# Three seven-product steps instead of two in the first seven column pairs, with the banks joined through transfers

## The chip, the cores and the metric

The kernel runs on one core of one Trainium2 chip. The metric is the device time of one execution in microseconds (us). Three executions of the kernel before took 2105.9 to 2107.35 us, with a median of 2106.39 us.

## The reference

The program is two transformer-like layers on 256 tokens of width 2048, in float32. The change touches only the first large projection, `proj = einsum('bsd,dn->bsn', rms_norm(x, norm_g), w_in)`: of its columns, the second half of `v_a`, then `o_a` and `z_a` (which gate the mLSTM output as `sigmoid(o_a) * h_a * silu(z_a)`), and `z_b` (used as `silu(z_b)`). Everything else (the remaining columns, the mLSTM, the attention, the Fourier mix, the MLP) is the same before and after.

## The kernel before

**Stream and pieces.** All weights arrive as a stream of units, each 128 partitions by 2048 columns (1 MB), through a ring of four buffers `raw` (SyncE, L477 to L479: unit u is asked for when the first two pieces of unit u-4 are split). A unit is cut into pieces of 1024 columns. ScalarE rounds a piece to the format that TensorE reads (`w_hi`, `split`, L1203), VectorE subtracts (`w_lo`, `split`, L1747), and TensorE multiplies activations with both: three matmuls of 128x512 for each product (`hi*hi`, `hi*lo`, `lo*hi`; `product`, L732 to L734). `w_hi` and `w_lo` have four places. Piece n may be rounded only when TensorE is done with piece n-4 (`act.wait_ge(w_used, ...)`, L1201). So ScalarE and VectorE are at most four pieces ahead of TensorE.

**Column pairs.** Seven pairs of 1024 columns each (`pair_in`, PAIRS_IN = 7) are computed in eight steps. One step is one unit, that is two k-tiles by two column halves, for two token tiles: eight block products. A plain step (`plain_step`, L742) has two pieces of 12 matmuls, 24 in all. A special step (`sum_step`, L754) is a Winograd step: seven products, 21 matmuls, in four pieces of 6, 3, 6 and 6 matmuls. The last step (`end_step`, L775) is plain, but ordered by bank. The results of a pair lie in four banks called whole and four called mixed; the roles swap from pair to pair (`parts_in`, L337). `SUM_AT_IN` says where the special steps are: steps 3 and 5 in pairs 1 to 4, steps 2 and 5 in pairs 0, 5 and 6.

**What a special step costs beside TensorE.** VectorE adds weights before it: `sum_weights` (L1753) makes one add of 1024 columns (L1761) and two of 512 (L1764, L1765), into one of two buffers `w_sum`. It is called inside `split`, directly after the first piece of the unit before. The special unit then has four pieces (1024, 512, 1024, 1024 columns) to round and to subtract, where a plain one has two of 1024. The sums of the activations (`xs_hi`, `xs_lo`) are made once, in the stage before (`sum_x`, `round_x_sums`, `rest_of_x_sums`).

**Joins.** In the step after the last special one, ScalarE copies the first mixed bank into `joined` (L1359) and VectorE makes four adds there (`join_mixed`, L2006 to L2011, two in each slot). At the end of the pair VectorE adds the four whole banks as they come (`join_whole`, L2023). In step 0 of the next pair ScalarE and VectorE turn `joined` into results (`take`): for pair 0 four scaled copies (`take_v`), for pairs 1 to 4 four sigmoids (L1326, L1328) and two pairs of VectorE products (`take_o`, L1977, L1978), for pairs 5 and 6 four sigmoids (L1337) and four products (`take_z`, L1989), where the sigmoids of the second half wait for the products of the first.

**Order.** Each engine works through its queue in program order. A `slot(j)` is run behind piece j's turn in the loop, and because the split is four pieces ahead, the slot of (step s, piece j) stands behind the split of the piece four further on. In this text piece s.j is piece j of step s of a pair. In pair 0 there are two extra slots: a table load and two sines on ScalarE at step 0 (L1351, L1352), and `rope_k` on VectorE at step 3 (L1844 to L1855). GpSimd (the POOL queue) has nothing to do during the pairs; behind them it stores `z1` (L509).

## Time and profile before

| | |
|---|---|
| median of three executions | 2106.39 us (2105.9 to 2107.35) |
| the profiled execution | 2106.43 us |
| its span, first to last instruction | 2104.2 us |
| granted TensorE clock | 0.999 of full |
| TensorE matmuls, busy | 2085.2 us, x10059 |
| VectorE busy | 1442.1 us |
| ScalarE busy | 1084.4 us |
| GpSimd busy | 39.6 us |

The span leaves 2.2 us of the profiled execution's time outside it. Matmuls overlap: one lasts 0.39 us from start to end while the next starts 0.23 us behind it, so the starts and not the busy time tell the pace. A column "[idle before <-releaser]" gives the time that the engine waited before an instruction and the work that ended the wait. In the timeline, "x3" is a run of three instructions shown as one, with the time from the first's start to the last's end.

### The profile page before, as it was taken

To read this page: it belongs to the slowest core of one execution; us is meant where nothing else is said; L and a number is where in the kernel's file an instruction comes from. 1 tells how busy PE (TensorE), PEld (TensorE's weight loads), DVE (VectorE), ACT (ScalarE), POOL (GpSimd) and SP (SyncE) were. 2 spreads that over 40 slices of the span, in tenths; PEclk is the share of its full clock that TensorE was granted. 3 is DMA by queue.
4 is the path that set the end of the run, shared out by engine and by line. 5 is a ranking of instruction groups with operands and counts; after the bars stand their busy time and mean duration, and the time that the engine had idled before them with its cause. 6 is when DMAs were issued, how large, how long until landed. Compare 5 with 4: busy or idle time off the path is not lost.

```text
span 2104.2 us, 24976 instructions
## 1 busy us (share of the span) xinstructions
PE 2085.2 (99%) x10059; PEld 1751.8 (83%) x10059; DVE 1442.1 (69%) x1872; ACT 1084.4 (52%) x1412; POOL 39.6 (2%) x49
## 2 busy tenths in 40 slices
PE   8999999999999999999999999999999999999998
PEld 6888888888888888888888888888888888888886
DVE  5977788875555786556554455466896796796684
ACT  5455555555444675554454454354544554454453
POOL 0000000000000020000000000000000000000000
PEclk9999999999999999999999999999999999999999
DMA  7555555564565544365755542455555465456562
GB/s 273 180 196 188 196 200 202 188 244 185 180 224 197 182 158 160 140 221 199 296 184 187 188 160 101 162 198 190 195 207 189 169 232 183 178 199 220 183 220 98
DMA packets 56803, 402.60 MB, mean 191 GB/s; under 512 B 6256, under 2 KB 6640, under 8 KB 9584
## 3 DMA queue, kind: packets, MB, share of 16 engines
q1 hardware_dynamic: 53648, 380.61, 50.3%
q0 software_dynamic: 2608, 19.66, 2.4%
q8 instruction: 80, 1.31, 0.3%
q10 hardware_dynamic: 432, 0.73, 0.1%
q14 instruction: 35, 0.29, 0.0%
HBM read 392.59 MB, written 8.39 MB: 191 GB/s over the span
## 4 chain that ended last, share of the span: by engine, by line
PE 96%; DVE 1%; ACT 1%; issue 1%; DMA 0%; SPq 0%; POOLq 0%; POOL 0%; DVEq 0%; ACTq 0%
PE proj L619 15%; PE proj L621 15%; PE proj L620 15%; PE proj L1092 11%; PE proj L1096 6%; PE proj L732 4%; PE proj L734 4%; PE proj L733 4%; PE tbank L732 2%; PE tbank L733 2%; PE tbank L734 2%; PE tbank L578 2%; PE bank_a L732 1%; PE bank_a L734 1%; PE bank_a L733 1%; PE bank_b L732 1%
## 5 line engine op out<-in xcount | busy, mean ns | idle before, releaser
L1747 DVE TENSOR_TENSOR w_lo<-raw,w_hi 128x1024 fp32r<-128x1024 f32 x630 | 747.1, 1200 | 517.0 <-ACT w_hi L1203 509.5
L1203 ACT ACTIVATE w_hi<-raw 128x1024 fp32r<-128x1024 f32 x630 | 647.9, 1040 | 745.7 <-PE proj L621 466.2
L619 PE MATMUL proj<-w_hi,a_both 128*128 128x512 f32 x1280 | 512.6, 401 | 0.0
L621 PE MATMUL proj<-w_hi,a_both 128*128 128x512 f32 x1280 | 500.3, 391 | 0.0
L620 PE MATMUL proj<-w_lo,a_both 128*128 128x512 f32 x1280 | 499.0, 390 | 0.0
L621 PEld LDWEIGHTS proj<-w_hi,a_both 128*128 128x128 f32 x1280 | 240.5, 188 | 51.8
L620 PEld LDWEIGHTS proj<-w_lo,a_both 128*128 128x128 f32 x1280 | 241.0, 188 | 47.5
L619 PEld LDWEIGHTS proj<-w_hi,a_both 128*128 128x128 f32 x1280 | 241.0, 188 | 47.0
L1092 PE MATMUL proj<-a_both,w_hi 128*128 128x512 f32 x672 | 160.6, 391 | 0.3 <-DVE a_both L1793 0.3
L1092 PEld LDWEIGHTS proj<-a_both,w_hi 128*128 128x128 f32 x672 | 123.5, 188 | 24.5 <-DVE a_both L1793 0.5
L1203 ACT ACTIVATE w_hi_deep<-raw 128x1024 fp32r<-128x1024 f32 x84 | 83.6, 1021 | 95.1 <-PE proj L1096 59.5
L1747 DVE TENSOR_TENSOR w_lo_deep<-raw,w_hi_deep 128x1024 fp32r<-128x1024 f32 x84 | 97.1, 1177 | 44.4 <-ACT w_hi_deep L1203 44.1
L1096 PEld LDWEIGHTS proj<-a_both,w_lo 128*128 128x128 f32 x672 | 86.3, 191 | 3.4
L1096 PE MATMUL proj<-a_both,w_lo 128*128 128x256 f32 x672 | 87.3, 283 | 0.0
L1092 PE MATMUL proj<-a_both,w_hi_deep 128*128 128x512 f32 x352 | 84.1, 391 | 0.0
L1092 PEld LDWEIGHTS proj<-a_both,w_hi_deep 128*128 128x128 f32 x352 | 64.7, 188 | 12.6
L732 PE MATMUL proj<-w_hi,a_both 128*128 128x512 f32 x164 | 64.0, 391 | 0.1
L733 PE MATMUL proj<-w_lo,a_both 128*128 128x512 f32 x164 | 63.8, 389 | 0.0
L734 PE MATMUL proj<-w_hi,a_both 128*128 128x512 f32 x164 | 63.8, 389 | 0.0
L1096 PEld LDWEIGHTS proj<-a_both,w_lo_deep 128*128 128x128 f32 x352 | 45.3, 191 | 1.8
L619 PE MATMUL proj<-w_hi,lat_hi 128*128 128x512 f32 x112 | 45.7, 408 | 0.3 <-DVE v_b L2251 0.3
L1096 PE MATMUL proj<-a_both,w_lo_deep 128*128 128x256 f32 x352 | 45.8, 283 | 0.0
(524 smaller groups left out, 2999.3 us busy)
## 6 DMA issues: line engine op xcount, KB each, us to landing
raw<-stream SPq DMA_DIRECT2D x358, 1024.0 KB, 4.8
nat<-x SPq DMA_DIRECT2D x4, 512.0 KB, 9.6
z_store<-z POOLq DMA_DIRECT2D x1, 2048.0 KB, 8.4
ga_store<-z POOLq DMA_DIRECT2D x1, 2048.0 KB, 12.1
gb_store<-z POOLq DMA_DIRECT2D x4, 512.0 KB, 7.2
yb<-z_store POOLq DMA_DIRECT2D x4, 512.0 KB, 9.6
ga<-ga_store POOLq DMA_DIRECT2D x1, 2048.0 KB, 8.1
gb<-gb_store POOLq DMA_DIRECT2D x1, 2048.0 KB, 14.3
```

Of the source, the lines that this page charges most:

```text
L578: last = nc.tensor.transpose(tbank[(tr.n - aside.n) % 2][:, b * P:(b + 1) * P], src(b), ident)
L619: nc.tensor.matmul(banks[t][:, :], ah, wh, start=first, stop=False)
L620: nc.tensor.matmul(banks[t][:, :], ah, wl, start=False, stop=False)
L621: last = nc.tensor.matmul(banks[t][:, :], al, wh, start=False, stop=end)
L732: nc.tensor.matmul(bank[:, :], hi, wh, start=first, stop=False)
L733: nc.tensor.matmul(bank[:, :], hi, wl, start=False, stop=False)
L734: return nc.tensor.matmul(bank[:, :], lo, wh, start=False, stop=end)
L1092: nc.tensor.matmul(banks[f], hi_places[place_of(piece.n + i)][:, cols], a_both[:, kt, :, :].rearrange("p s t -> p (s t)"), start=(kt == 0) ...
L1096: last = nc.tensor.matmul(banks[f][:, 0:TOK], lo_places[place_of(piece.n)][:, cols], a_hi[:, kt, :], start=False, stop=(kt == KT - 1))
L1203: A(hi_places[s][:, 0:width], src, ACT.Copy).then_inc(w_rounded, 1)
L1747: V.tensor_tensor(lo_places[s][:, 0:width], src, hi_places[s][:, 0:width].bitcast(f32), SUB).then_inc(w_rest, 1)
```

## The change

There are three special steps in each of the seven pairs, at steps 1, 3 and 5, and a third set of activation sums, made in the second `v` projection before the pairs. `w_sum` has one buffer instead of two during the pairs. The mixed banks are joined in one go in step 5 (the slot of its third piece): ScalarE waits for all four pieces of the step, copies one bank, and VectorE makes the four additions, now with signs such that the whole banks need only be added. `join_whole` is gone from VectorE. In its place ScalarE copies the four whole banks into `stg` and `stg2` (`drain_pair`), and GpSimd issues four transfers that add these to `joined` in memory (`accum_op=ADD`), 28 in all. The `take` of the pair before moves from step 0 to step 2 on ScalarE, where it waits for the four transfers, and on VectorE to step 2 (second slot, first half) and step 4 (first slot, second half). Behind the last pair it moves from pieces 0 and 1 of the next projection to pieces 3 and 4. The diff, with repeated hunks (the removed waits on `whole_added` in `take_o` and `take_z`, the indexing of `xs_hi` and `xs_lo`) left out:

```diff
...
 PAIRS_IN = 7
-GROUPS_IN = (1, 4)
-SUM_AT_IN = [(2, 5)] + [(3, 5)] * 4 + [(2, 5)] * 2
-ORDER_IN = [(0, 2, 1, 3, 5, 4, 6, 7) if at[0] == 2 else (0, 2, 3, 1, 5, 4, 6, 7) for at in SUM_AT_IN]
+GROUPS_IN = (1, 4, 5)
+SUM_AT_IN = [(1, 3, 5)] * PAIRS_IN
+ORDER_IN = [(0, 1, 2, 4, 3, 5, 6, 7)] * PAIRS_IN
 def _sum_units():
...
 SUM_UNITS = _sum_units()
-SUMS_IN = 2 * PAIRS_IN
+SUMS_IN = len(GROUPS_IN) * PAIRS_IN
 def _pieces():
...
         joined = place("joined", [P, 4, CW], f32, 152.25)
-        w_sum_vo = place("w_sum_vo", [P, 2, 2 * PIECE], f32, 160.25)
-        w_sum_z = place("w_sum_z", [P, 2, 2 * PIECE], f32, 176.25)
+        xs_hi_2 = place("xs_hi_2", [P, 4, P], f32r, 176.25)
+        xs_lo_2 = place("xs_lo_2", [P, 4, P], f32r, 178.25)
+        xs_hi = [xs_hi[:, 0], xs_hi[:, 1], xs_hi_2[:, :, :]]
+        xs_lo = [xs_lo[:, 0], xs_lo[:, 1], xs_lo_2[:, :, :]]
+        w_sum_vo = place("w_sum_vo", [P, 2 * PIECE], f32, 160.25)
+        w_sum_z = place("w_sum_z", [P, 2 * PIECE], f32, 184.25)
...
         at += 8
+        drain_in = {2: stg[:, 0, :], 3: stg[:, 1, :], 0: stg2[:, 0, :], 1: stg2[:, 1, :]}
...
         def w_sums(i):
-            if i < 2 * 5:
-                return w_sum_vo[:, i % 2, :]
-            return (w_sum_z if i < SUMS_IN else w_sum)[:, i % 2, :]
+            if i < SUMS_IN:
+                return (w_sum_vo if i < len(GROUPS_IN) * 5 else w_sum_z)[:, :]
+            return w_sum[:, i % 2, :]
         def par_c(name, i=0):
...
         m_copied = sem("m_copied")
-        whole_added = sem("whole_added")
+        joined_in = [sem(f"joined_in{o}") for o in range(4)]
...
+            for p in range(PAIRS_IN):
+                for i, o in enumerate(END_ORDER):
+                    pool.wait_ge(part_read, 5 * p + 2 + i)
+                    pool.dma_start(joined[:, o, :], drain_in[o], accum_op=ADD).then_inc(joined_in[o], 16)
...
             def take_v(p, n):
-                act.wait_ge(whole_added, 4 * (p + 1))
                 for t in range(TT):
...
             def take(p, n):
                 if p >= 0:
+                    if n == 0:
+                        for o in END_ORDER:
+                            act.wait_ge(joined_in[o], 16 * (p + 1))
                     (take_v if p < 1 else take_o if p < 5 else take_z)(p, n)
...
+            def drain_pair(p):
...
+                act.wait_ge(part_read, 5 * p + 1)
+                if p == 0:
+                    act.wait_ge(qk_ready, 8)
+                act.wait_ge(gated, tiles.at(2))
+                for i, o in enumerate(END_ORDER):
+                    if i < 3:
+                        act.wait_ge(part_done, 3 * p + i + 1)
+                    else:
+                        act.wait_ge(w_used, done.at(RING + 2))
+                    A(drain_in[o], parts_in[p % 2][o][:, :], ACT.Copy).then_inc(part_read, 1)
             def pair_in(p):
...
                             A(cos[:, :, :], cos[:, :, :], ACT.Sin).then_inc(trig, 1)
-                        if step == 0:
+                        if step == 2:
                             take(p - 1, j)
-                        if step == SUM_AT_IN[p][-1] + 1 and j == 0:
-                            act.wait_ge(w_used, done.at(RING))
+                        if step == SUM_AT_IN[p][-1] and j == 2:
+                            act.wait_ge(w_used, done.at(RING + 4))
...
                             A(joined[:, 0, :], parts_in[1 - p % 2][0][:, :], ACT.Copy).then_inc(m_copied, 1)
+                    if step == STEPS - 1:
+                        drain_pair(p)
...
                 chunk.add(2)
...
+            def last_x_sums(j):
+                if j == 6:
+                    act.wait_ge(qk_ready, 8)
+                    round_x_sums(2)
...
             for i in range(2):
-                pieces(slot=(lambda j: (conv_slot(j), exp_slot(j))) if i == 0 else lambda j: exp_slot(8 + j))
+                pieces(slot=(lambda j: (conv_slot(j), exp_slot(j))) if i == 0 else lambda j: (exp_slot(8 + j), last_x_sums(j)))
                 for t, b in enumerate(banks()):
...
             for i in range(2):
                 def lat_slot(j, i=i):
-                    if i == 0 and j < 2:
-                        take(PAIRS_IN - 1, j)
-                    if i == 0 and j == 4:
+                    if i == 0 and 3 <= j < 5:
+                        take(PAIRS_IN - 1, j - 3)
+                    if i == 0 and j == 7:
                         act.wait_ge(gated, tiles.at(2))
+                        act.wait_ge(proj_read, chunk.at() * 2)
...
                 s = w_sums(i).rearrange("p (b c) -> p b c", b=4)
-                if i > 1:
-                    dve.wait_ge(w_rest, FIRST_PIECE[SUM_UNITS[i - 2]] + 4)
+                reader = i - (1 if i < SUMS_IN else 2)
+                if reader >= 0 and (i < SUMS_IN) == (reader < SUMS_IN):
+                    dve.wait_ge(w_rest, FIRST_PIECE[SUM_UNITS[reader]] + 4)
...
-            def take_o(n):
...
-                if n == 0:
-                    return
+            def take_o(t):
...
                 i = tiles.n // 2
-                for t in range(TT):
-                    tiles.add()
-                    dve.wait_ge(sig, tiles.at())
-                    chain(V.tensor_tensor(stg2[:, t, :], stg2[:, t, :], stg[:, t, :], MUL))
-                    V.scalar_tensor_tensor(nat[:, t, i * CW:(i + 1) * CW], joined[:, 2 * t + 1, :], inv1[:, t:t + 1],
-                                           stg2[:, t, :], MUL, MUL).then_inc(gated, 1)
-                    dve.wait_ge(gated, tiles.at(2))
-                    dve.sem_inc(proj_read, 1)
+                tiles.add()
+                dve.wait_ge(sig, tiles.at())
+                chain(V.tensor_tensor(stg2[:, t, :], stg2[:, t, :], stg[:, t, :], MUL))
+                V.scalar_tensor_tensor(nat[:, t, i * CW:(i + 1) * CW], joined[:, 2 * t + 1, :], inv1[:, t:t + 1],
+                                       stg2[:, t, :], MUL, MUL).then_inc(gated, 1)
+                dve.wait_ge(gated, tiles.at(2))
+                dve.sem_inc(proj_read, 1)
             def take_z(n):
...
-            def take(p, n):
+            def take(p, half):
                 if p >= 1:
-                    (take_o if p < 5 else take_z)(n)
+                    (take_o if p < 5 else take_z)(half)
             def join_mixed(p, part):
...
                     chain(V.tensor_tensor(m[:, 2, :], mixed[2][:, :], m[:, 0, :], ADD))
-                    V.tensor_tensor(m[:, 1, :], mixed[1][:, :], m[:, 2, :], ADD).then_inc(dve_seq, 1)
+                    V.scalar_tensor_tensor(m[:, 1, :], mixed[1][:, :], -1.0, m[:, 2, :], MUL, SUB).then_inc(dve_seq, 1)
...
                 else:
-                    chain(V.tensor_tensor(m[:, 2, :], mixed[3][:, :], m[:, 2, :], ADD))
-                    V.tensor_tensor(m[:, 3, :], mixed[1][:, :], m[:, 2, :], ADD).then_inc(part_read, 1)
...
-            def join_whole(p):
...
-                whole = parts_in[p % 2]
-                dve.wait_ge(dve_seq, seq.at())
-                dve.wait_ge(part_read, 5 * p + 1)
-                for i, o in enumerate(END_ORDER):
-                    if i < 3:
-                        dve.wait_ge(part_done, 3 * p + i + 1)
-                    else:
-                        dve.wait_ge(w_used, done.at(RING + 2))
-                    V.tensor_tensor(joined[:, o, :], whole[o][:, :], joined[:, o, :],
-                                    SUB if o in (1, 2) else ADD).then_inc(part_read, 1)
-                dve.wait_ge(part_read, 5 * p + 5)
-                dve.sem_inc(whole_added, 4)
+                    dve.wait_ge(dve_seq, seq.at())
+                    chain(V.scalar_tensor_tensor(m[:, 2, :], mixed[3][:, :], -1.0, m[:, 2, :], MUL, SUB))
+                    V.tensor_tensor(m[:, 3, :], mixed[1][:, :], m[:, 2, :], SUB).then_inc(part_read, 1)
             def pair_in(p):
...
                     def slot(j):
...
                             rope_k()
-                        if step == 0:
-                            take(p - 1, j)
-                        if step == at[-1] + 1:
-                            join_mixed(p, j)
-                    if step == STEPS - 1:
-                        join_whole(p)
+                        if step == 2 and j == 1:
+                            take(p - 1, 0)
+                        if step == 4 and j == 0:
+                            take(p - 1, 1)
+                        if step == at[-1] and j == 2:
+                            join_mixed(p, 0)
+                            join_mixed(p, 1)
...
                 gates_slot(8 * i + j)
+                if i == 1 and j == 5:
+                    sum_x(2)
+                if i == 1 and j == 7:
+                    rest_of_x_sums(2)
...
             for i in range(2):
                 def lat_slot(j, i=i):
-                    if i == 0 and j < 2:
-                        take(PAIRS_IN - 1, j)
-                        if j:
+                    if i == 0 and 3 <= j < 5:
+                        take(PAIRS_IN - 1, j - 3)
+                        if j == 4:
...
```

## Rows read from the trace of the kernel before

**Rows 1.** The page: engines, and the chain that ended last

```profile
PE 2085.2 (99%) x10059; PEld 1751.8 (83%) x10059; DVE 1442.1 (69%) x1872; ACT 1084.4 (52%) x1412; POOL 39.6 (2%) x49
...
PE 96%; DVE 1%; ACT 1%; issue 1%; DMA 0%; SPq 0%; POOLq 0%; POOL 0%; DVEq 0%; ACTq 0%
```

**Rows 2.** Busy time by stretch, each about one pair (columns in the first line)

```profile
core 0: us, PE busy (x) PEld busy (x) DVE busy (x) ACT busy (x) POOL busy (x), PEclk, DMA share, GB/s
...
284.00:326.00 42.00, 41.93 (x185) 34.41 (x184) 34.91 (x38) 22.98 (x25) 0.00 (x0) 1.00 0.52 195
326.00:369.00 43.00, 42.93 (x189) 35.21 (x188) 35.92 (x40) 22.97 (x25) 0.00 (x0) 1.00 0.53 200
```

**Rows 3.** Waits from 200 to 455 us: total us, times, longest

```profile
DVE w_lo L1747 <- ACT w_hi L1203: 38.9, 34, 2.5
ACT w_hi L1203 <- PE bank_b L734: 17.8, 4, 4.4
ACT stg L1337 <- DVE z L1989: 2.8, 1, 2.8
```

**Rows 4.** TensorE's timeline: first of 49 matmuls without gap, then a gap

```profile
297.09 0.39 PE L734 MATMUL proj<-w_hi,a_both 128*128 128x512 f32 x1
...
307.97 0.39 PE L734 MATMUL proj<-w_hi,a_both 128*128 128x512 f32 x1
308.43 0.50 PE L732 MATMUL proj<-w_hi,a_both 128*128 128x512 f32 x1
308.77 0.39 PE L733 MATMUL proj<-w_lo,a_both 128*128 128x512 f32 x1
309.00 0.39 PE L734 MATMUL proj<-w_hi,a_both 128*128 128x512 f32 x1
```

**Rows 5.** Idle time in front of TensorE's L732, 200 to 700 us

```profile
  DVE w_lo L1747: 2.3, 5
```

**Rows 6.** VectorE's timeline in pair 2, with the take of pair 1

```profile
292.20 1.22 DVE L1747 TENSOR_TENSOR w_lo<-raw,w_hi 128x1024 fp32r<-128x1024 f32 x1
293.33 0.69 DVE L1977 TENSOR_TENSOR stg<-stg,stg 128x512 f32<-128x512 f32 x1
294.06 0.75 DVE L1978 SCALAR_TENSOR_TENSOR nat<-joined,inv,stg 128x512 f32<-128x512 f32 x1
294.95 0.69 DVE L1977 TENSOR_TENSOR stg<-stg,stg 128x512 f32<-128x512 f32 x1
...
304.57 1.22 DVE L1761 TENSOR_TENSOR w_sum_vo<-raw 128x1024 f32<-128x1024 f32 x1
...
307.16 2.96 DVE L1747 TENSOR_TENSOR w_lo<-raw,w_hi 128x1024 fp32r<-128x1024 f32 x3
...
314.00 4.63 DVE L1747 TENSOR_TENSOR w_lo<-raw,w_hi 128x1024 fp32r<-128x1024 f32 x4
320.12 1.23 DVE L1747 TENSOR_TENSOR w_lo<-raw,w_hi 128x1024 fp32r<-128x1024 f32 x1 [1.49 <-ACT w_hi L1203]
321.26 0.69 DVE L2006 TENSOR_TENSOR joined<-tbank,joined 128x512 f32<-128x512 f32 x1
321.98 0.69 DVE L2007 TENSOR_TENSOR joined<-bank_b,joined 128x512 f32<-128x512 f32 x1
...
325.43 2.48 DVE L2023 TENSOR_TENSOR joined<-proj,joined 128x512 f32<-128x512 f32 x4
```

**Rows 7.** ScalarE's timeline in the same pair

```profile
288.34 1.32 ACT L1326 ACTIVATE stg<-joined,inv 128x512 f32<-128x512 f32 x2
...
302.33 3.10 ACT L1203 ACTIVATE w_hi<-raw 128x1024 fp32r<-128x1024 f32 x3 [0.30 <-PE proj L734]
...
308.45 1.06 ACT L1203 ACTIVATE w_hi<-w_sum_vo 128x1024 fp32r<-128x1024 f32 x1 [2.14 <-PE proj L734]
...
319.99 0.58 ACT L1359 ACTIVATE joined<-bank_a 128x512 f32<-128x512 f32 x1
```

**Rows 8.** The extra slots of pair 0: ScalarE's table load, VectorE's rope

```profile
163.47 1.28 ACT L1351 ACT_TABLE_LOAD   x1
164.76 0.26 ACT L1351 ACTIVATE sin<-sin 128x64 f32<-128x64 f32 x1
164.92 0.24 ACT L1352 ACTIVATE cos<-cos 128x64 f32<-128x64 f32 x1
...
179.04 0.29 DVE L1844 TENSOR_TENSOR kr<-sm 128x128 f32<-128x128 f32 x1
...
181.32 0.69 DVE L1747 TENSOR_TENSOR w_lo<-raw,w_hi 128x512 fp32r<-128x512 f32 x1
```

**Rows 9.** VectorE's timeline, 459 to 465 us: take behind the last pair

```profile
459.19 1.64 DVE L1989 SCALAR_TENSOR_TENSOR z<-joined,inv,stg 128x512 f32<-128x512 f32 x2
460.98 1.22 DVE L1747 TENSOR_TENSOR w_lo<-raw,w_hi 128x1024 fp32r<-128x1024 f32 x1
...
464.00 1.23 DVE L1747 TENSOR_TENSOR w_lo<-raw,w_hi 128x1024 fp32r<-128x1024 f32 x1 [0.24 <-DVE z L1989]
```

**Rows 10.** A GpSimd issue; transfers by line (KB each, us to landing)

```profile
464.22 0.58 POOL L509 DMA_DIRECT2D z_store<-z  x1 [431.74 <-DVEq L2065]
...
raw<-stream SPq DMA_DIRECT2D x358, 1024.0 KB, 4.8
...
gb_store<-z POOLq DMA_DIRECT2D x4, 512.0 KB, 7.2
yb<-z_store POOLq DMA_DIRECT2D x4, 512.0 KB, 9.6
...
out<-nat SPq DMA_DIRECT2D x2, 256.0 KB, 2.9
```

More of the change, by code:

```diff
@@ L804, in pair_in @@
                         i = at.index(step)
-                        sum_step(kt, whole, mixed, a_hi, a_lo, xs_hi[:, i], xs_lo[:, i], i + 1, i == 0, i == len(at) - 1)
+                        sum_step(kt, whole, mixed, a_hi, a_lo, xs_hi[i], xs_lo[i], i + 1, i == 0, i == len(at) - 1)
                     elif step == STEPS - 1:
@@ L1291, in round_x_sums @@
                 act.wait_ge(ms_summed, i + 1)
-                A(xs_hi[:, i, :, :], xs[:, :, :], ACT.Copy).then_inc(ms_rounded, 1)
+                A(xs_hi[i], xs[:, :, :], ACT.Copy).then_inc(ms_rounded, 1)
             def k_slot(j, i):
@@ L1320, in take_o @@
             def take_o(p, n):
-                act.wait_ge(whole_added, 4 * (p + 1))
                 for t in range(TT):
@@ L1332, in take_z @@
             def take_z(p, n):
-                act.wait_ge(whole_added, 4 * (p + 1))
                 for t in range(TT):
@@ L1953, in rest_of_x_sums @@
                 dve.wait_ge(ms_rounded, i + 1)
-                V.tensor_tensor(xs_lo[:, i, :, :], xs[:, :, :], xs_hi[:, i, :, :].bitcast(f32), SUB).then_inc(ms_rest, 1)
+                V.tensor_tensor(xs_lo[i], xs[:, :, :], xs_hi[i].bitcast(f32), SUB).then_inc(ms_rest, 1)
             def k_slot(j, i):
```

## The prediction

> **What bounds the kernel now.** I read the page first. TensorE is busy for 99% of the span and is 96% of the chain that ended last [rows 1]. That does not yet say that it never waits, since matmuls overlap, so the second view is the busy time by stretch: in a stretch of one pair VectorE is busy 35 to 36 of 42 to 43 us, ScalarE 23, and the transfers 53% [rows 2]. The third is the table of waits: almost all waits of ScalarE are on TensorE and those of VectorE on ScalarE, and both are harmless, since they only mean that the ring of four pieces is full [rows 3]. The last are the timelines. TensorE starts a matmul every 10.88 / 48 = 0.2267 us [rows 4]. A plain step is then 24 x 0.2267 = 5.44 us, a piece of it 2.72, a special step 21 x 0.2267 = 4.76 (pieces of 1.36, 0.68, 1.36, 1.36).
>
> TensorE does wait in a few places: five times, 2.3 us with the 0.2267 us of pace that each gap between starts contains [rows 5], so 2.3 - 5 x 0.2267 = 1.2 us, and 0.11 more each for the restart (0.34 where the pace is 0.23) [rows 4]. One such gap is from 307.97 to 308.43, behind w_lo of the second piece of plain step 4, which stands between special steps 3 and 5. VectorE could not start that piece before 307.16, since the weight sums of step 5 (from 304.57, 2.59 us) stand in front of it [rows 6]. So **a plain step between two special ones already costs TensorE 0.23 + 0.11 = 0.34 us**. The change makes two such places in each pair and puts further work in them.
>
> **What is removed.** One plain step in seven pairs becomes special: 7 x 3 matmuls x 0.2267 = 4.76 us. The four gaps of pairs 1 to 4 and a small one in pair 6 go too, as pieces of the old order: 4 x 0.34 + 0.15 = 1.5 us. Both together, 6.3 us, are what can be gained. VectorE loses four adds at the pair's end (2.48 us) [rows 6]. They hold up nothing: VectorE waits for ScalarE right behind them [rows 3], so their end gains nothing by itself.
>
> **What is added, piece by piece.** Lengths: ScalarE starts a rounding 0.25 us behind TensorE's end of the piece it waits for (308.45 against 307.97 + 0.2267) and takes 1.06, or about 1.01 with another behind it [rows 7]. VectorE takes 1.23 behind a wait, 1.14 in a row (4.63 = 3 x 1.14 + 1.22), 2.59 for the three sums [rows 6]. From its end to TensorE's next matmul I take 0.09; the gap at 308.43 against 307.16 + 1.23 shows 0.04 [rows 4, 6], and I add as much for the hops between the queues.
>
> (a) *Step 2, behind special step 1, pairs 1 to 6.* From TensorE's end of piece 1.0: 0.25 + 1.06 (ScalarE, 2.0) + 1.14 (VectorE, 2.0) + 2.59 (sums for step 3) + 1.23 (VectorE, 2.1) + 0.09 = 6.36. TensorE has 0.68 + 1.36 + 1.36 + 2.72 = 6.12 us of work. Missing: 0.24, with the restart 0.35, which is the gap seen before. Six times: 2.1 us.
>
> (b) *Step 4, behind special step 3, pairs 2 to 5.* Piece 3.3 may be rounded when TensorE ends 2.1. VectorE's queue then holds 3.3, the first tile of the moved take (0.73 + 0.89 = 1.62, from 293.33 to 294.95 [rows 6]), 4.0, the sums for step 5, and 4.1. Piece 4.0: 0.25 + 1.06 + 1.14 + 1.62 + 1.23 + 0.09 = 5.39 against 4.76 of step 3: 0.63 + 0.11. Then 4.1 needs 2.59 + 1.14 = 3.73 behind 4.0, while TensorE works on 4.0 for 2.72: another 1.01. Together 1.75, four times: 7.0 us. In pair 1 the take is ScalarE's alone (1.32 [rows 7] between 3.3 and 4.0): 0.25 + 1.01 + 1.32 + 1.06 + 1.23 + 0.09 = 4.96, so 0.31 + 1.01 = 1.3 us.
>
> (c) *Pair 0.* The table load and the sines (163.47 to 165.16, 1.7 us [rows 8]) stand behind the split of 1.3, in front of 2.0. From TensorE's end of 0.1: 0.25 + 1.01 + 1.7 + 1.06 + 1.23 + 0.09 = 5.34 against 4.76, so 0.69, and 1.01 for 2.1: 1.7 us. rope_k (179.04 to 181.32, 2.28 us) stands behind the sums for step 5, in front of 4.1: 0.24 + 2.28 + 0.11 = 2.6 us.
>
> (d) *Pair 6.* Here ScalarE's second pair of sigmoids waits for VectorE's first two products, as it already did once for 2.8 us with plain pieces as cover [rows 3]. From the end of 2.1: 0.25 + 1.06 + 1.14, two products (1.79, from 459.19 to 460.98 [rows 9]), two sigmoids 1.34, then 4.0 on ScalarE 1.06 and VectorE 1.23, 0.09: 8.0 against 4.76, so 3.3 us with the restart, and again 1.01 for 4.1: 4.3 us.
>
> (e) *The join.* ScalarE's wait for the whole of step 5 costs nothing, since its next piece needs the same. The copy (0.58) and four VectorE operations (0.72 each, 321.26 to 321.98 [rows 6, 7]) stand in front of the second piece of step 7, with 5.44 us of step 6 as cover. With VectorE some 0.5 us behind at that point I get 5.6: about 0.13 a pair, 0.9 us in all, and nothing if VectorE has caught up.
>
> (f) *The drain.* Four ScalarE copies lie where ScalarE idled 4.4 us [rows 3]. The last delays piece 1.0 of the next pair: 0.25 + 0.64 + 1.06 + 1.23 + 0.09 = 3.3 us against the 5.44 of step 0: covered. So are the third activation sums, in plain pieces with 1.5 us of idle VectorE each [rows 6]. The single sum buffer adds no wait, its readers stand earlier in VectorE's own queue. If that cover went, each would cost its excess only.
>
> (g) *The transfers.* No row shows one that adds. ScalarE needs them behind its rounding of 3.2, which waits for TensorE's end of 2.0: 5.44 + 4.76 + 2.72 + 0.25 + 1.01 = 14.2 us behind the pair's end; and the last is issued by 1.6 us (0.9 for the drained bank, 0.6 to 0.7 for the issue), so it has 12.6 us. The nearest plain ones take 2.9 us (256 KB) and 7.2 to 9.6 (512 KB, from GpSimd) [rows 10]. I take something between, 5 us, which costs nothing, with the ends zero and what rival B gives. Weight transfers land in 4.8 us and have some 13 us, so contention must nearly treble that to matter. One row speaks on whether VectorE keeps GpSimd from issuing: its issue at 464.22 took 0.58 us while VectorE ran a w_lo from 464.00 to 465.23, and neither is longer than usual [rows 9, 10].
> The Trainium skill, page "SBUF — State Buffer", section "SBUF: two separate sides", states that GpSimd writes the descriptors of its transfers and can be shut out while VectorE runs a two-port operation; with the page's 3.1 us instead of 0.62 for an issue, four would end near 13 us and the joins would come at the limit, which would add rival B's time. That trace row does not agree, though it is one issue.
>
> **Sum.** 2.1 + 7.0 + 1.3 + 1.7 + 2.6 + 4.3 + 0.9 = 19.9 us added, 6.3 removed: 13.6 us slower. The profiled execution took 2106.43 us (span 2104.2, 2.2 outside), the median is 2106.39, so the same base: **2120 us**. The terms' own uncertainty, 0.1 us for each of 28 stops, the 0.9 of (e), and a third of (c) and (d), gives 2115 to 2125.
>
> **Rivals.** A, *not slower: the takes are hidden.* Everything hangs on whether VectorE's work between TensorE's end of 2.1 and the end of w_lo of 4.1 (9.1 us in pairs 2 to 5) fits in 7.5 us. If it did, because the queue is further ahead than my count of four pieces says, only the bare gap would stay: 14 x 0.35 - 1.5 - 4.76 = -1.4, 2105.0 us. For it: VectorE's work in a pair, 3 x 4.0 + 5 x 2.28 (splits) + 3 x 2.59 (sums) + 2.9 (join) + 3.2 (take) = 37.3 us, is less than the pair's 5 x 5.44 + 3 x 4.76 = 41.5; and the takes cost nothing before. Against it: the ring of four is a wait in the code, and the bare gap is in the trace. If the bare gap were hidden as well, -4.8 - 1.5 gives 2100.1 us, *faster*. B, *joins arrive late.* If the last transfer takes 16 us instead of under 12.6, ScalarE stands 3.4 us in each of six pairs in front of the stall that is already there: +20 us, 2140. For it: four transfers at once among 200 GB/s of weights, a second read for the sum. Against: every GpSimd row of 512 KB lands under 10 us. C, *the gain is smaller than 21 matmuls*, because a special step issues some other way: the same code runs in 14 steps of the trace, so under 1 in 100.
>
> **How the numbers follow.** Forecast 0.74; A with only the takes hidden 0.09; all hidden 0.05; B 0.12. Two tenths of a per cent (4.2 us) is about what a measurement of this kernel tells from no change. The forecast and B are slower by more, A is within it, all hidden is faster: 0.05, 0.09, 0.86. The range takes in the forecast's own 2115 to 2125, on the low side a case in which three fifths of what (b) to (d) add beyond seven bare gaps (16.9 - 2.4 = 14.5 us) is hidden (2111), on the high side the half of B that is late by under 2 us (2130). Left out are A's two cases and the later half of B, 0.2.
>
> **What would show it.** 21 fewer TensorE matmuls than 10059. A pair's length from its last drained bank to the next's: about 45.9 (pair 0), 43.3, 43.7 four times, 46.4 (pair 6) instead of 42.5 or 42.1. VectorE's w_lo as the releaser of TensorE's L732 in some 28 places instead of 5, the longest (3 us) in pair 6 and (2.5 us) at rope_k. ScalarE's idle time in front of the takes released by TensorE, not by a DMA; if a DMA stands there, B holds. Pairs of 41.5 us and no more than 5 gaps would make the prediction wrong.

## The result, and the profile after

The changed kernel took 2122.18 us (median of 4 runs, 2121.81 to 2122.63) beside 2106.8 us for the kernel before on the same chip (4 runs, 2105.9 to 2107.35): a ratio of 1.0074, with a 95% interval from 1.0062 to 1.0086. That is 15.4 us slower; 13.6 were forecast, and 2122.18 lies in the range. The profiled execution took 2122.63 us, of which the span is 2120.7. Of the executions of the last batch below, two of the kernel before and two of e11 were slow ones, at 2555 to 9618 us, and its medians are those of the others.

The page of the changed kernel: the engines' busy time, the chain that ended last, and two of its DMA issues (KB each, median us to landing).

```profile
PE 2089.1 (99%) x10038; PEld 1748.5 (82%) x10038; DVE 1455.6 (69%) x1885; ACT 1110.3 (52%) x1455; POOL 63.4 (3%) x77
...
PE 93%; DVE 3%; ACT 2%; issue 2%; DMA 0%; SPq 0%; POOLq 0%; DVEq 0%; POOL 0%; ACTq 0%
...
raw<-stream SPq DMA_DIRECT2D x358, 1024.0 KB, 4.8
joined<-stg POOLq DMA_DIRECT2D x28, 256.0 KB, 7.4
```

TensorE issues 21 matmuls fewer than in [rows 1], as the change says, and still its busy time has grown by 3.9 us. Part of the chain has moved from TensorE to VectorE and ScalarE: from 1% each to 3% and 2%. Transfers have 0% of it.

Where TensorE stops is told by the idle time in front of L741, the first matmul of each triple. For the same stretch as [rows 5] (200 to 700 us) the row is the first below; the second fence has the waits from 160 to 470 us, all seven pairs (us in total, times, longest).

```profile
  DVE w_lo L1777: 26.9, 34
```

```profile
ACT w_hi L1212 <- PE tbank L743: 58.7, 35, 5.9
DVE w_lo L1777 <- ACT w_hi L1212: 50.9, 35, 3.0
...
PEld bank_a L741 <- DVE w_lo L1777: 14.0, 11, 3.3
PE bank_a L741 <- DVE w_lo L1777: 9.1, 8, 2.9
...
PEld proj L741 <- DVE w_lo L1777: 8.0, 12, 1.1
...
PE proj L741 <- DVE w_lo L1777: 3.2, 6, 0.7
...
ACT stg L1343 <- DVE z L2017: 2.9, 1, 2.9
...
PEld tbank L741 <- DVE w_lo L1777: 0.9, 4, 0.2
```

The first two rows only say that the ring is full, as in [rows 3]. A longer stop is listed twice, once in front of the weight load (PEld) and once in front of the matmul (PE). The weight loads alone are 11 + 12 + 4 = 27 stops, against 5 before. They sum to 22.9 us, less 27 x 0.2267 us of pace, 16.8 us. No row names a DMA.

The stops themselves, as the distance between starts less 0.2267 us, come from TensorE's timeline. Behind each stop the next start is 0.11 us late as well (the restart), so a stop is written as 0.63 + 0.11. Around pair 3, whose like before had no stop but the one in [rows 4]:

```profile
305.28 0.39 PE L743 MATMUL proj<-w_hi,a_both 128*128 128x512 f32 x1
305.74 0.50 PE L741 MATMUL proj<-w_hi,a_both 128*128 128x512 f32 x1
...
314.00 0.50 PE L741 MATMUL proj<-w_hi,a_both 128*128 128x512 f32 x1 [0.47 <-DVE w_lo L1777]
...
317.72 0.50 PE L741 MATMUL proj<-w_hi,a_both 128*128 128x512 f32 x1 [0.70 <-DVE w_lo L1777]
```

The first is at piece 2.1 (0.23 us, and 0.11 more behind the next matmul for the restart), the second at 4.0 (0.63 + 0.11, with the matmul before it at 313.14), the third at 4.1 (0.86 + 0.11, matmul before at 316.63). VectorE's timeline shows what stood in front of the two later ones:

```profile
309.95 1.23 DVE L1777 TENSOR_TENSOR w_lo<-w_sum_vo,w_hi 128x1024 fp32r<-128x1024 f32 x1 [1.39 <-ACT w_hi L1212]
311.10 0.68 DVE L2005 TENSOR_TENSOR stg<-stg,stg 128x512 f32<-128x512 f32 x1
311.82 0.75 DVE L2006 SCALAR_TENSOR_TENSOR nat<-joined,inv,stg 128x512 f32<-128x512 f32 x1
312.72 1.23 DVE L1777 TENSOR_TENSOR w_lo<-raw,w_hi 128x1024 fp32r<-128x1024 f32 x1
313.86 1.22 DVE L1792 TENSOR_TENSOR w_sum_vo<-raw 128x1024 f32<-128x1024 f32 x1
315.11 0.69 DVE L1795 TENSOR_TENSOR w_sum_vo<-w_sum_vo,raw 128x512 f32<-128x512 f32 x1
315.84 0.69 DVE L1796 TENSOR_TENSOR w_sum_vo<-w_sum_vo,raw 128x512 f32<-128x512 f32 x1
```

The split of 3.3, the moved take (two operations), the split of 4.0, the sums for step 5, and only then the split of 4.1, from 316.44: the queue that step (b) of the prediction wrote down.

Two stops are longer, at rope_k in pair 0 and at the sigmoids of pair 6. Busy time by stretch around them (columns in the first line). The first row is the stop at rope_k, the second the 4.3 us behind it, the third the time after that, the fourth the 4.3 us behind the stop of pair 6; the last is pair 3 as a whole, which answers to [rows 2]:

```profile
core 0: us, PE busy (x) PEld busy (x) DVE busy (x) ACT busy (x) POOL busy (x), PEclk, DMA share, GB/s
181.00:184.60 3.60, 1.28 (x6) 0.74 (x4) 3.36 (x12) 1.06 (x1) 0.00 (x0) 1.00 0.00 0
184.70:189.00 4.30, 4.30 (x12) 3.40 (x13) 2.75 (x3) 0.00 (x0) 0.00 (x0) 0.61 0.77 272
189.10:193.00 3.90, 3.90 (x19) 3.19 (x18) 2.39 (x3) 3.27 (x4) 0.00 (x0) 1.00 0.58 231
447.60:451.90 4.30, 4.30 (x12) 3.39 (x13) 4.23 (x5) 1.08 (x2) 0.00 (x0) 0.60 0.00 0
283.40:327.10 43.70, 42.45 (x184) 34.02 (x183) 36.98 (x40) 26.50 (x31) 3.40 (x4) 1.00 0.66 216
```

In pair 3 TensorE now idles for 1.25 of 43.70 us, where [rows 2] have 0.07. The column PEclk is what the prediction did not have: over the 4.3 us behind each stop the granted clock is 0.6 in the mean (it is 0.50 from 185.7 to 189.0 us, while the slow matmuls run), and 12 matmuls fit in 4.3 us where 19 fit in 3.9 us a moment later. The timeline has it matmul by matmul:

```profile
181.89 0.39 PE L743 MATMUL tbank<-w_hi,a_both 128*128 128x512 f32 x1
184.63 0.50 PE L741 MATMUL bank_a<-w_hi,a_both 128*128 128x512 f32 x1 [2.36 <-DVE w_lo L1777]
184.98 0.40 PE L742 MATMUL bank_a<-w_lo,a_both 128*128 128x512 f32 x1
...
185.70 0.63 PE L742 MATMUL bank_b<-w_lo,a_both 128*128 128x512 f32 x1
186.13 0.63 PE L743 MATMUL bank_b<-w_hi,a_both 128*128 128x512 f32 x1
186.56 0.63 PE L741 MATMUL tbank<-w_hi,a_both 128*128 128x512 f32 x1
```

A stop of 2.51 us, four matmuls at the old pace, and then eight with 0.43 us between starts instead of 0.2267: 8 x 0.2 = 1.6 us more. The slow spacing is that of the lower of the two levels, 1.2 GHz instead of 2.4 (512 / 1.2 GHz = 0.427 us). This is one reason why PE's busy time grew; the longer first matmul behind each stop (0.50 us instead of 0.39) is another.

**The account.** What all distances between starts in the seven pairs have over 0.2267 us, slow matmuls included, sums to 22.8 us in the changed kernel and to 1.6 in the kernel before. With 4.76 us for the removed matmuls the pairs are 16.4 us longer. The two profiled spans differ by 16.5 us (2120.7 and 2104.2), so outside the pairs the time is the same within 0.2 us; the medians differ by 15.4. Of the 22.8 us the rows below hold 22.0; the other 0.8 is in distances that are less than 0.05 us too long each.

| step of the prediction | forecast, us | found, us |
|---|---|---|
| (a) six stops at 2.1 | 2.1 | 6 x 0.35 = 2.1 |
| (b) 4.0 and 4.1 in pairs 1 to 5 | 8.3 | 1.42 + 2.23 + 3 x 1.72 = 8.8 |
| (c) pair 0: sines, 2.1 | 1.7 | 0.64 + 0.97 = 1.6 |
| (c) pair 0: rope_k | 2.6 | 2.6, slow matmuls 1.6: 4.2 |
| (d) pair 6: sigmoids, 4.1 | 4.3 | 3.1 + 0.1, slow matmuls 1.5: 4.7 |
| (e) join | 0.9 | about 0.6 |
| removed | -6.3 | -4.8 and -1.6 |

### The profile page after: what moved, and what is told of

Read it like the earlier page. It is cut to its first block, busy times and chain, and to the rows that moved or that the text cites. A ratio compares the mean times of both kernels' runs of the same rounds, so it can differ in the third digit from the quotient of the medians.

```text
span 2120.7 us, 25046 instructions
## 1 busy us (share of the span) xinstructions
PE 2089.1 (99%) x10038; PEld 1748.5 (82%) x10038; DVE 1455.6 (69%) x1885; ACT 1110.3 (52%) x1455; POOL 63.4 (3%) x77
## 4 chain that ended last, share of the span: by engine, by line
PE 93%; DVE 3%; ACT 2%; issue 2%; DMA 0%; SPq 0%; POOLq 0%; DVEq 0%; POOL 0%; ACTq 0%
PE proj L628 15%; PE proj L630 15%; PE proj L629 15%; PE proj L1101 11%; PE proj L1105 6%; PE proj L741 4%; PE proj L743 3%; PE proj L742 3%; PE tbank L741 2%; PE tbank L742 2%; PE tbank L743 2%; PE tbank L587 2%; PE bank_a L741 1%; PE bank_a L742 1%; PE bank_a L743 1%
## 5 line engine op out<-in xcount | busy, mean ns | idle before, releaser
L1101 PEld LDWEIGHTS proj<-a_both,w_hi_deep 128*128 128x128 f32 x352 | 64.8, 188 | 12.6
L741 PE MATMUL proj<-w_hi,a_both 128*128 128x512 f32 x150 | 59.7, 398 | 3.5 <-DVE w_lo L1777 3.2
L1212 ACT ACTIVATE w_hi<-w_sum_vo 128x1024 fp32r<-128x1024 f32 x30 | 31.8, 1060 | 56.4 <-PE tbank L743 35.8
L1777 DVE TENSOR_TENSOR w_lo<-w_sum_vo,w_hi 128x1024 fp32r<-128x1024 f32 x30 | 36.7, 1223 | 23.5 <-ACT w_hi L1212 23.1
```

What stands on the lines that cost most here:

```text
L741: nc.tensor.matmul(bank[:, :], hi, wh, start=first, stop=False)
L1101: nc.tensor.matmul(banks[f], hi_places[place_of(piece.n + i)][:, cols], a_both[:, kt, :, :].rearrange("p s t -> p (s t)"), start=(kt == 0) ...
L1212: A(hi_places[s][:, 0:width], src, ACT.Copy).then_inc(w_rounded, 1)
L1777: V.tensor_tensor(lo_places[s][:, 0:width], src, hi_places[s][:, 0:width].bitcast(f32), SUB).then_inc(w_rest, 1)
```

## The experiments

All but e7 start from the changed kernel, and all compute the reference's whole result. Each batch ran beside the kernel before on one chip; its medians were 2106.56 us (e1 to e4), 2106.66 (e5 to e8) and 2107.01 (e10 to e12). A ratio is to that.

**e1: rope_k four steps later.** Of pair 0's long stop only the slot is changed: VectorE runs rope_k behind piece 1.0 of the next pair instead of 4.0.

```
-                        if p == 0 and step == 3 and j == 0:
+                        if p == 0 and step == 7 and j == 0:
                             rope_k()
```

> Only rope_k in pair 0 moves, from VectorE's slot at step 3 to the one at step 7. Queue theory (each stop of TensorE is the excess of VectorE's and ScalarE's queued work over the four pieces of cover): the 2.5 us stop in front of piece 4.1 shrinks to the bare 0.97, no 1.6 us of slow matmuls follow it, the rest stays: 2122.2 - 4.0 = about 2118 us, pair 0 about 43.6 us from drain to drain. If the slow matmuls came with something else in pair 0 and not with the long stop, 2119.7. Rival (the transfers and GpSimd cost the time): 2122, unchanged.

Measured: 2118.63 us, ratio 1.0058 (1.0044 to 1.0071). Of the 15.4 us 3.3 are gone; in the trace pair 0 is 3.9 us shorter. The stop at 4.1 has not stayed at 0.97 us as I had thought but shrunk to 0.23 + 0.11, since pair 0 has no take that would put VectorE behind at 4.0. The same 4.3 us of time as above, which now hold the matmuls of step 5:

```profile
184.70:189.00 4.30, 4.30 (x20) 3.57 (x19) 2.77 (x4) 3.47 (x4) 0.00 (x0) 1.00 0.96 360
```

The clock is at 1.00, and no matmul of pair 0 is slow any more. So the slow matmuls belong to the stop, not to this place in the program: they are gone with it.

**e2: the join back on VectorE.** The four drains and the four transfers go, VectorE's four adds come back, all else stays. This is the test of what the change does with GpSimd.

```
-            for p in range(PAIRS_IN):
-                for i, o in enumerate(END_ORDER):
-                    pool.wait_ge(part_read, 5 * p + 2 + i)
-                    pool.dma_start(joined[:, o, :], drain_in[o], accum_op=ADD).then_inc(joined_in[o], 16)
...
-                    if step == STEPS - 1:
-                        drain_pair(p)
...
+                    if step == STEPS - 1:
+                        join_whole(p)
```

> Three special steps as in the change, but the four whole banks are added on VectorE at the pair's end as before, with no ScalarE drain and no adding transfers. Queue theory: both kinds of join lie under the cover of step 0, so 2122 us within 1. Rival (the transfers take port, DMA or ScalarE time that TensorE misses): 2117 us or less.

Measured: 2122.32 us, ratio 1.0075 (1.0062 to 1.0089), the same as the change's. TensorE's stops stand at the same places with the same sizes (rope 2.53, pair 6 3.02, then 0.24, 0.63 and 0.83 to 0.87 in pairs 3 to 5). The drain through transfers costs nothing and brings nothing: the VectorE time that it frees stands at the pair's end, where VectorE waited anyway.

**e3: the takes earlier.** The slots count the piece that TensorE works on, four behind the one prepared. ScalarE's takes move from behind 3.2 and 3.3 to behind 3.0 and 3.1, VectorE's from behind 3.3 and 5.2 to behind 3.1 and 5.0, and only the first two sigmoids of a take still wait for VectorE's products.

```
-                    act.wait_ge(gated, tiles.at(2))
+                    if n == 0:
+                        act.wait_ge(gated, tiles.at(2))
...
-                        if step == 2:
-                            take(p - 1, j)
+                        if (step, j) in ((1, 2), (1, 3)):
+                            take(p - 1, ((1, 2), (1, 3)).index((step, j)))
...
-                        if step == 2 and j == 1:
-                            take(p - 1, 0)
-                        if step == 4 and j == 0:
-                            take(p - 1, 1)
+                        if (step, j) in ((1, 3), (3, 2)):
+                            take(p - 1, ((1, 3), (3, 2)).index((step, j)))
```

> The takes move: ScalarE to step 1, third and fourth slot (joins have landed by then), VectorE's first tile to step 1, fourth slot, the second to step 3, third slot, that is away from the places in front of the sums; and in pairs 5 and 6 the second two sigmoids no longer wait for the first two products, since they write another buffer. Queue theory: step 4 goes from 1.7 us a pair to at most the bare 0.35, pair 6 loses its 3.1 us stop and the slow matmuls: 2106.8 + 5 = about 2112 us. Rival (it is the third step's mass of splits and sums, not the takes): at most 2 us less than 2122.

Measured: 2110.94 us, ratio 1.0021 (1.0012 to 1.003). Eleven of the 15.4 us are gone, of which the sigmoids' edit alone brings 1.9 (e6 below). What is left are two stops of some 0.35 us in each of pairs 1 to 6, and in pair 0 the two behind the sines (0.53 and 0.83, with 0.11 each) and the rope stop, with its slow matmuls.

**e5 and e7: the sums behind the second piece.** The sums stand behind the split of a step's first piece, and so in front of its second one. In e5 they move behind the second piece in the changed kernel; e7 does the same to the kernel before.

```
-                    if u + 1 in SUM_UNITS and piece.n == FIRST_PIECE[u]:
+                    if u + 1 in SUM_UNITS and piece.n == FIRST_PIECE[u] + (u + 1 in SUM_UNITS[:SUMS_IN]):
                         sum_weights(u + 1)
```

> The change with one edit: in the pairs VectorE makes the weight sums behind the second piece of the unit before, not the first. Queue theory: the 1.0 us stops of the second pieces (4.1) go, since they are the sums' 2.6 us against 2.7 of cover less a split; the stops of 4.0 behind the takes, the 3 us stop of pair 6 and a part of rope_k's stay: about 2106.6 + 9 = 2116 us. Rival (the order of sums and splits does not matter, only their amount): 2122.

> The kernel before with the weight sums of the pairs behind the second piece of the unit before. Queue theory: the four gaps of 0.34 us in pairs 1 to 4 go, a new small one may come in one pair: 2106.6 - 1.0 = 2105.6 us. Rival (these gaps are matmul restarts of another cause): 2106.6.

Measured: e5 2115.2 us, ratio 1.0041 (1.0027 to 1.0055); e7 2105.35 us, 0.9993 (0.9985 to 1.0002). In e5 the stop at 2.1 is gone; the one of 0.63 at 4.0 stays, since the take makes it, and the one of 0.86 has become two of 0.34 to 0.38 further on. More than half of the gain is in pair 0, which is 4.2 us shorter in the trace: the sums no longer stand with rope_k in front of 4.1, a stop of 0.85 + 0.11 at 5.0 is left of the 2.51, and no matmul behind it is slow. In e7 the idle time in front of TensorE's first matmul of a triple, over the whole kernel, is down from [rows 5] to

```profile
  DVE w_lo L1747: 0.3, 1
```

The four gaps of [rows 4] are gone, worth 4 x 0.34 = 1.4 us by the trace; 1.3 were measured, which the interval does not tell from nothing. They were made by the sums, as the prediction read them.

**e6: the second sigmoids don't wait.** Only the first edit of e3.

```
-                    act.wait_ge(gated, tiles.at(2))
+                    if n == 0:
+                        act.wait_ge(gated, tiles.at(2))
```

> The change with one edit: in pairs 5 and 6 the second two sigmoids no longer wait for the first two products. Queue theory: the 3.0 us stop in pair 6 falls to 0.7 or less and the slow matmuls behind it go; a bare 1.0 us stop of the next piece comes back in their place. Pair 6 from 46.9 to about 44 us: 2122.2 - 2.9 = 2119.3 us. Rival (that wait is covered): 2122.

Measured: 2120.15 us, ratio 1.0063 (1.005 to 1.0077): 1.9 of the 15.4 us are gone, where I expected 2.9; in the traces the gaps of the pairs fall by 2.7. In the changed kernel ScalarE waits 2.87 us for VectorE's products, with 4.0 behind it (ScalarE's timeline, then TensorE's):

```profile
443.99 1.33 ACT L1343 ACTIVATE stg<-joined,inv 128x512 f32<-128x512 f32 x2 [2.87 <-DVE z L2017]
```

```profile
447.58 0.50 PE L741 MATMUL bank_a<-w_hi,a_both 128*128 128x512 f32 x1 [2.85 <-DVE w_lo L1777]
```

In e6 TensorE's timeline has two short stops of 0.81 and 0.83 us in their place, and no slow matmul behind them:

```profile
445.56 0.50 PE L741 MATMUL bank_a<-w_hi,a_both 128*128 128x512 f32 x1 [0.65 <-DVE w_lo L1778]
...
449.28 0.50 PE L741 MATMUL bank_a<-w_hi,a_both 128*128 128x512 f32 x1 [0.67 <-DVE w_lo L1778]
```

**e4 and e10: all of it together.** e4 has the edits of e1, e3 and e5; e10 also moves pair 0's sines from behind 1.3 to behind 5.2.

```
-                        if p == 0 and step == 0 and j == 1:
+                        if p == 0 and step == 4 and j == 0:
                             act.wait_ge(trig_arg, 2)
```

> e1 and e3 together, and the weight sums stand behind the second piece of the unit before instead of behind the first. Queue theory: with the sums one piece later the bare 0.35 us gap at steps 2 and 4 closes too; what stays is about 0.35 in two places in pairs 2 to 5 and the table load of pair 0: 2106.8 - 1.5 = about 2105 us, the change's 4.76 us then shows in part. Rival (VectorE's 90% is itself the limit): 2110 us or more.

> e4 with one more edit: the table load and the sines of pair 0 stand at step 4 instead of step 0. Queue theory: the 0.53 + 0.11 us stop in front of piece 2.0 of pair 0 goes, nothing else moves: e4's 2104.8 - 0.7 = 2104.1 us.

Measured: e4 2104.84 us, ratio 0.9992 (0.9983 to 1.0001); e10 2104.21 us, 0.9987 (0.9978 to 0.9996). The idle time in front of L741, over the whole kernel, is 35.3 us in 41 rows for the changed kernel and here, e4 first and then e10:

```profile
  DVE w_lo L1778: 7.3, 19
```

```profile
  DVE w_lo L1778: 6.0, 17
```

With three special steps, the early join and the transfers all kept, but the other work put where a piece has cover, the change (e10) is faster than the kernel before by 2.8 us: less than the 6.3 that it removes, since 4.0 us of gaps are left, mostly stops of some 0.15 + 0.11 us twice a pair from pair 2 on. But part of the 2.8 us is not the change's: e7 moves the sums alone and gains 1.3. The gaps of the pairs sum to 0.1 us in e7 and to 4.0 in e10, so by the traces the change itself brings 4.76 - 3.9 = 0.9 us over a kernel before with its sums moved too, and the intervals of e7 and e10 overlap: that it pays is not shown.

**e8, e12, e11: other special steps.** e8 keeps the transfers and puts the special steps at 1, 3 and 6, so that the join comes later, the takes, sines, rope_k and sums at places with cover. e12 is e8 with e2's join on VectorE. e11 has the steps 2, 4 and 6, also with that join.

```
-SUM_AT_IN = [(1, 3, 5)] * PAIRS_IN
-ORDER_IN = [(0, 1, 2, 4, 3, 5, 6, 7)] * PAIRS_IN
+SUM_AT_IN = [(1, 3, 6)] * PAIRS_IN
+ORDER_IN = [(0, 1, 2, 4, 3, 6, 5, 7)] * PAIRS_IN
...
-                        if step == 2:
-                            take(p - 1, j)
+                        if (step, j) in ((1, 2), (2, 0)):
+                            take(p - 1, ((1, 2), (2, 0)).index((step, j)))
```

> The version that the queue theory puts first: as e4, but with the special steps at 1, 3 and 6 (two plain steps between the second and the third), the join in step 6, the table load of pair 0 at step 4, ScalarE's takes at step 1, third slot, and step 2, first, VectorE's at step 3, first and third slot. Queue theory: 2106.6 - 3.0 = 2103.6 us, faster than e4 by 1.2. Rival (the later join in step 6 collides with the drain and the next pair's start): 2106 us or more.

> e8 with one edit: the whole banks are joined on VectorE, no drain and no adding transfers. In e8 ScalarE waited 23 us for transfers that landed after up to 14 us. If these waits are what made e8 slow, the stops of TensorE behind them go, though VectorE's four adds now stand in its queue: 2106.6 + 1.5 = 2108 us, no slow matmuls in pair 1. Rival (e8's loss is the late join in step 6 itself): 2113.7 as e8, or more.

> Three special steps at 2, 4 and 6, whole banks joined on VectorE without transfers, sums behind the second piece, ScalarE's takes at step 0, second slot, and step 1, first; VectorE's at step 1, first slot, and step 3, first. No transfer can be late here. Queue theory: 2106.6 - 2.9 = 2103.7 us, the fastest of all. Rival (a special step 6 pushes VectorE's join and adds into the next pair's start, as e8 may have suffered): 2108 us or more.

Measured: e8 2113.68 us, ratio 1.0033 (1.0021 to 1.0045), ten above what I expected; e12 2109.03 us, 1.0011 (1.0001 to 1.002); e11 2104.01 us, 0.9987 (0.9978 to 0.9997), with one stop of 0.37 + 0.11 us a pair. The waits of e8, 160 to 470 us, have what those of the changed kernel lacked:

```profile
ACT stg L1366 <- DVE joined L2041: 17.6, 7, 2.5
ACT stg L1333 <- DMA joined<-stg: 11.5, 3, 4.6
...
ACT L1333 <- DMA joined<-stg: 5.4, 1, 5.4
ACT stg L1344 <- DMA joined<-stg: 3.6, 1, 3.6
```

The cause is in the timeline of ScalarE and GpSimd, and in the query of the transfers' line:

```profile
239.92 1.58 ACT L1366 ACTIVATE stg<-proj 128x512 f32<-128x512 f32 x3 [2.52 <-DVE joined L2041]
240.82 3.45 POOL L516 DMA_DIRECT2D joined<-stg  x4 [39.37 <-ACT stg L1366]
...
257.14 1.28 ACT L1333 ACT_TABLE_LOAD   x1 [5.38 <-DMA joined<-stg]
```

```profile
DMA to landing us min/median/max: 7.6/10.1/14.3
```

The join of step 6 now ends just before the drain, the first drain waits 2.5 us for it, all four come in a row, and so do the four transfers. In the changed kernel they are issued 1.4 us apart and land in

```profile
DMA to landing us min/median/max: 3.3/7.4/10.5
```

This is rival B, transfers that come late, in a kernel that I made so. e8 less e12, each to its own kernel before, is 7.0 - 2.0 = 5.0 us: that is the difference between the two joins. The late transfers cost more than that, since e12's join on VectorE makes stops that e8 lacks, at piece 1.0 (0.43 to 0.48 us, pairs 1 to 6) and at 1.1 of pair 1 (1.43 us, where rope_k stands as well). Common to both is a stop of 0.37 + 0.11 us in front of 7.0 in each pair, 3.4 us in all, which my expectation of 2103.6 had at nothing.

## Why the prediction was right

**The reading of the bound** held. TensorE set the time, a stop was a late split of VectorE, and VectorE's average of 69% busy said nothing of it. e3 and e5 move VectorE's and ScalarE's work without taking any away, and give 11.0 and 6.9 us back. The pairs took 47.5, 43.4, 44.3, three times 43.7 and 46.7 us, where 45.9, 43.3, four times 43.7 and 46.4 were forecast.

The chain of causes was right, and the sum came out 1.8 us low with errors of both signs, named below, so that a part of its closeness is luck. That the gaps are the whole cost holds beyond the change: summed from each run's trace as above, less the 1.6 + 4.76 us of the kernel before, they give the differences of the ten kernels made from the changed one to within 0.1 to 1.4 us.

**(a)** was exact: 0.34 or 0.35 us, six times; e5 takes them out. **(b)** forecast 0.63 + 0.11 and 1.01 in pairs 3 to 5; the trace has 0.63 + 0.11 and 0.86 + 0.11. Pair 2 has 1.13 in place of 0.63. The 0.5 is a term that I left out: its first sigmoid needs another table, and ScalarE's timeline shows the load behind the rounding of 3.2; that of 3.3 has to wait for it and the sigmoids.

```profile
261.46 1.06 ACT L1212 ACTIVATE w_hi<-w_sum_vo 128x1024 fp32r<-128x1024 f32 x1 [2.15 <-PE tbank L743]
262.54 1.28 ACT L1333 ACT_TABLE_LOAD   x1
263.84 1.34 ACT L1333 ACTIVATE stg<-joined,inv 128x512 f32<-128x512 f32 x2
```

**(c)** was right for the sines. For rope_k the stop was right (2.51 + 0.11 for 2.6), but its price was not: the 1.6 us of slow matmuls behind it are missing. **(d)** has the same error of 1.5 us, and one against it: the 1.01 us at 4.1 came as 0.09 only. The slow matmuls of 4.0 gave VectorE 1.5 us more to catch up, and e6 agrees: there the clock stays up and the stop at 4.1 is there, 0.83 us. The terms that were mis-sized are therefore these two: I priced a stop by its length alone. Over both, the clock costs 3.1 us less the 0.9 of that stop with its restart: 2.2, more than the 1.8 by which the whole forecast was low.

**(e)** was 0.06 to 0.09 a pair for 0.13. **(f)** and **(g)** were right at zero, which e2 shows as a whole. A transfer took 7.4 us in the median instead of the 5 that I took, and 10.5 at the longest, inside the 12.6 that it had; the margin is thin, as e8 shows.

The Trainium skill's rule on GpSimd's descriptors (page "SBUF — State Buffer", section "SBUF: two separate sides") is about VectorE operations in a two-port mode; an operation with two SBUF inputs, it says, stands only against a GpSimd operation that reads SBUF. The w_lo in [rows 9] and all VectorE operations beside the 28 issues are of the second kind, so the prediction was wrong to hold its row against the page: the page asks for no delay there, and none is seen. The page's 3.1 us, too, are for a whole transfer and not for the issue. GpSimd's timeline, and VectorE's:

```profile
290.95 0.85 POOL L516 DMA_DIRECT2D joined<-stg  x1 [0.44 <-ACT stg L1365]
292.31 0.85 POOL L516 DMA_DIRECT2D joined<-stg  x1 [0.51 <-ACT stg L1365]
```

```profile
290.58 1.22 DVE L1777 TENSOR_TENSOR w_lo<-raw,w_hi 128x1024 fp32r<-128x1024 f32 x1
```

The first issue lies wholly under a VectorE split of two inputs, the second beside an idle VectorE; both take 0.85 us, and none of the 28 more than 0.93.

**The rivals.** A fell: the takes are not hidden in the change, and e3 shows that it is their slots that cost. B fell for the change, and stands for e8. C fell: the removed 4.76 us close the account. What I did not foresee is that the loss can be undone with the change kept: e10 is faster than the kernel before, though not shown to be faster than e7. What is lost is lost by the places of the other work. Open is how to get rid of e10's last 4.0 us of gaps; an order without its 0.15 us stops was not tried.

## What to carry to other kernels

When a piece of work on the bounding engine is made shorter, list for each following piece what stands in the feeding engines' queues between the release of its buffer and its own preparation, and compare the sum with the cover that is left; averages of busy time don't show this. Before a change is given up as slower, try it with the side work moved: here that was worth 18 us, from 15.4 slower to 2.8 faster. And give the kernel before the same rearrangement where it can take it, or the gain is put down to the wrong edit: the moved sums alone gave it 1.3 us.

## What was unexpected of the hardware

**A stop of 2.5 us costs half as much again.** After stops of 2.51 us and 3.01 us TensorE's granted clock was 0.6 in the mean of 4.3 us, and eight or seven matmuls came at 0.43 us, which with one in between cost 1.6 and 1.5 us. After the stops of up to 1.13 us in the change it did not fall. In e8 one of 2.55 us, with another of 0.62 us close behind, brought it again (0.65 in the 4.3 us behind), and one of 1.43 us in e12 did not. What lies between 1.43 and 2.51 us no run shows. In the change the fall came 1.1 us behind the restart; in e2, at stops of the same length, the second start behind the restart was already late by more than the usual 0.11 us. The Trainium skill (page "TensorE: Matmul & The Clock Gate", section "Wait — 56ns, not 53.3ns?") states 0.4267 us between matmuls of 512 columns at the low level, and the trace agrees with 0.43; at the high level it states 0.2157, and this trace has 0.2267.

**Adding transfers come late when issued together.** 256 KB from SBUF to SBUF with an add landed in 3.3 to 10.5 us when issued 1.4 us apart, and in 7.6 to 14.3 us when four were issued in a row, where a plain store of the same size at the kernel's end, from SyncE's queue, took 2.9 us [rows 10]. The DMA share of pair 3 was 0.66, so this is the time among the weights; it was not measured alone, and e8 also moved the transfers to another time, so that the cause is not separated.
